# V/K stage: each turn of modulation rows is joined to the next block's first two chunks

## What is computed

```python
m = silu(c) @ w_ada + b_ada                  # (2048) @ (2048, 6*2048): shift, scale, gate, twice
h = rms_norm(x, g_pre) * (1.0 + scale) + shift
z = h @ w_in                                 # (2048, 4096): q | k | v | u
q, k = rotary(q), rotary(k)
attn = diff_attend(q, k, v, ...)             # prompt, and samples over cached pages
pooled = pool_mix(u, ...)
m = concatenate([rms_norm(attn) * ..., pooled]) @ w_out
x = x + gate * rms_norm(m, g_post)
x = x + gate2 * rms_norm(square(relu(h2 @ w1)) @ w2, g_post2)
```

## Time and profile before

| | |
|---|---|
| median of 3 runs | 1468.08 us (1467.49 to 1468.85) |
| profiled execution | 1467.77 us |
| its span | 1466.1 us |
| TensorE busy, share of the span | 1433.8 us, 98% |
| VectorE busy | 814.9 us, 56% |
| ScalarE busy | 524.8 us, 36% |
| bytes moved by DMA | 319.06 MB, mean 218 GB/s |
| mean granted TensorE clock | 0.995 |

### The profile page before, as it was taken

One profiled execution on the slowest core, in us unless ns is written; L12 is line 12 of the kernel. 1 busy time (PEld: TensorE's weight loads), 2 busy tenths in 40 slices (PEclk: granted clock), 3 DMA queues, 4 the chain that ended last, 5 costly groups with the idle time before them and its releaser, 6 DMA issues.

```text
span 1466.1 us, 26898 instructions
## 1 busy us (share of the span) xinstructions
PE 1433.8 (98%) x10278; PEld 1316.6 (90%) x10278; DVE 814.9 (56%) x1312; ACT 524.8 (36%) x753; POOL 115.4 (8%) x195
## 2 busy tenths in 40 slices
PE   6999999999999999999999999999999999999996
PEld 2788877888688879999999999999999999999996
DVE  5667668757555678664434554343554334555554
ACT  4333243443435644333222333332333322333331
POOL 1111000266210000000000000000000000000002
PEclk9999999999999999999999999999999999999998
DMA  9999888787799777334346334446443443334421
GB/s 374 342 340 341 331 311 314 276 310 281 282 349 347 280 269 300 144 143 172 143 165 238 144 143 157 159 144 239 156 151 144 152 161 146 144 143 144 149 109 72
DMA packets 88459, 319.06 MB, mean 218 GB/s; under 512 B 12240, under 2 KB 12496, under 8 KB 87744
## 3 DMA queue, kind: packets, MB, share of 16 engines
q1 hardware_dynamic: 79776, 290.49, 53.4%
q0 software_dynamic: 5360, 25.14, 4.6%
q10 hardware_dynamic: 3248, 2.39, 0.5%
HBM read 312.18 MB, written 5.80 MB: 217 GB/s over the span
## 4 chain that ended last, share of the span: by engine, by line
PE 93%; DVE 3%; DMA 1%; POOL 1%; issue 1%; ACT 1%; SPq 0%; POOLq 0%; ACTq 0%; DVEq 0%
PE bank L1572 74%; PE bank L1625 8%; PE bank L1549 3%; PE bank L1534 2%; PE bank L1897 2%; DMA raw<-in_stream 1%; PE bank L1812 1%; DVE w_lo L812 1%; PE bank L1743 1%; PE bank L1559 0%; PE bank L1842 0%; PE bank L1698 0%; PE bank L1524 0%; SPq L371 0%; ACT w_hi L418 0%
## 5 line engine op out<-in xcount | busy, mean ns | idle before, releaser
L418 ACT ACTIVATE w_hi<-raw 128x1024 fp32r<-128x1024 f32 x352 | 361.6, 1053 | 271.8 <-PE bank L1572 232.0
L812 DVE TENSOR_TENSOR w_lo<-raw,w_hi 128x1024 fp32r<-128x1024 f32 x352 | 419.6, 1226 | 40.9 <-ACT w_hi L418 38.6
L1572 PE MATMUL bank<-m_hi,w_hi 128*128 128x320 f32 x1280 | 397.2, 310 | 0.0
L1572 PE MATMUL bank<-m_hi,w_lo 128*128 128x320 f32 x1280 | 395.5, 309 | 0.0
L1572 PE MATMUL bank<-m_lo,w_hi 128*128 128x320 f32 x1280 | 395.5, 309 | 0.0
L1572 PE MATMUL bank<-h_hi,w_hi 128*128 128x320 f32 x1216 | 378.7, 311 | 0.0
L1572 PE MATMUL bank<-h_hi,w_lo 128*128 128x320 f32 x1216 | 375.7, 309 | 0.0
L1572 PE MATMUL bank<-h_lo,w_hi 128*128 128x320 f32 x1216 | 375.7, 309 | 0.0
L1572 PEld LDWEIGHTS bank<-m_hi,w_hi 128*128 128x128 f32 x1280 | 240.3, 188 | 12.0 <-issue 12.0
L1572 PEld LDWEIGHTS bank<-h_hi,w_hi 128*128 128x128 f32 x1216 | 228.3, 188 | 13.9 <-issue 13.8
L1572 PEld LDWEIGHTS bank<-m_lo,w_hi 128*128 128x128 f32 x1280 | 240.3, 188 | 0.0
(11 more groups left out here) (240 smaller groups left out, 1130.3 us busy)
## 6 DMA issues: line engine op xcount, KB each, us to landing
raw<-in_stream SPq DMA_DIRECT2D x544, 512.0 KB, 4.3
k_pages<-in_kc POOLq DMA_DIRECT2D x16, 512.0 KB, 6.4
v_pages<-in_vc POOLq DMA_DIRECT2D x16, 512.0 KB, 5.4
x<-in_x_cm SPq DMA_DIRECT2D x4, 640.0 KB, 6.8
x_mid<-in_x_cm POOLq DMA_DIRECT2D x1, 2560.0 KB, 10.0
x<-in_x_cm POOLq DMA_DIRECT2D x1, 2560.0 KB, 13.8
v_out<-v_cm POOLq DMA_DIRECT2D x1, 1280.0 KB, 9.5
k_out<-back POOLq DMA_DIRECT2D x1, 1280.0 KB, 6.0
```

Source lines behind the costliest of these rows:

```text
L418: act.activation(w_hi[2 * (j % 2) + h][:, :], raw[slot][:, h * 1024:(h + 1) * 1024], ACT.Copy).then_inc(hi_ready, 1)
L812: dve.tensor_tensor(w_lo[q][:, :], raw[slot][:, h * 1024:(h + 1) * 1024], w_hi[q][:, :], ALU.subtract).then_inc(slot_used[slot], 1)
L1572: last = pe.matmul(bank[j % 2][:, 0:T], w[q][:, k * P:(k + 1) * P], v[:, 8 * h + k, :], start=(h == 0 and k == 0 and n == 0), stop=(h == 1 ...
```

## The change

The turn of block n + 1 and chunks 0 and 1 of block n + 2 become one visit. TensorE's order in slice n after: V half 0; chunks 2 and 3 of block n + 1; V half 1 whole; turn of block n + 1 and chunks 0 and 1 of block n + 2 (in the last slice: and the first chunk of block 9); K half 0; K half 1. Block 1's first two chunks now lie before the first slice. The stream is laid out to match: block 0, chunks 0 and 1 of block 1, then for each slice the V chunk, chunks 2 and 3, the K chunk, chunks 0 and 1 of the block after. `keep_clock` before the stage has 4 matmuls, not 8.

```diff
-SLICED = [0, 3, 6, 9]
-SLICED_ADA = [[1, 2, 4, 5], [7, 8, 10, 11]]
+SLICED = [2, 5, 8, 11]
+SLICED_ADA = [[3, 4, 6, 7], [9, 10, 12, 13]]
...
-            ada_copy(n + 1, quarter_use(n // 2), SLICED_ADA[n % 2][3])
+            ada_copy(n + 1, quarter_use(n // 2), SLICED_ADA[n % 2][1])
...
         ada_turn(0)
-        keep_clock(bank[5], 8)
+        keep_clock(bank[5], 4)
+        for a in range(2):
+            ada_chunk(1, quarter_use(0), a, a)
...
                 nb, places = 2 * g + (i + 1), SLICED_ADA[i]
-                ada_chunk(nb, use, places[0], 0)
-                ada_chunk(nb, use, places[1], 1)
                 pe.wait_ge(h_ready, 2 * g + (i + 1))
                 slice_tiles(i, 0, 0, range(4))
-                slice_tiles(i, 0, 1, range(2))
-                ada_chunk(nb, use, places[2], 2)
-                ada_chunk(nb, use, places[3], 3)
-                slice_tiles(i, 0, 1, range(2, 4))
+                ada_chunk(nb, use, places[0], 2)
+                ada_chunk(nb, use, places[1], 3)
+                slice_tiles(i, 0, 1, range(4))
                 ada_turn(nb)
-                slice_tiles(i, 1, 0, range(4))
-                slice_tiles(i, 1, 1, range(2))
                 if last and i == 1:
                     nb, place, a = fill_ada(0)[0][0]
                     ada_chunk(nb, fill(0)[1], place, a)
-                slice_tiles(i, 1, 1, range(2, 4))
+                else:
+                    ada_chunk(nb + 1, use, places[2], 0)
+                    ada_chunk(nb + 1, use, places[3], 1)
+                slice_tiles(i, 1, 0, range(4))
+                slice_tiles(i, 1, 1, range(4))
...
-    chunks = ada_block(0)
-    for g in range(QUARTERS):
-        products = [slice_chunk(w_in, 2 * g + i, vk[8 * jj:8 * jj + 8]) for i in range(2) for jj in range(2)]
-        chunks += place(products, SLICED, (2 * g + 1, 2 * g + 2))
+    chunks = ada_block(0) + ada_block(1)[:2]
+    for n in range(SLICES):
+        chunks += [slice_chunk(w_in, n, vk[:8])] + ada_block(n + 1)[2:] + [slice_chunk(w_in, n, vk[8:])]
+        if n + 1 < SLICES:
+            chunks += ada_block(n + 2)[:2]
```

## The result

The changed kernel takes 1469.62 us (median of 20 runs, 1467.96 to 1472.23), the kernel before 1468.07 us (20 runs, 1466.61 to 1471.46). The forecast was 1470.4 us, 0.16% more.

The account below looks back on a forecast made before the run. TensorE, carrying 93% of the chain, bounds the kernel. Profiled 1467.77 us plus 2.3 lost at the stage's start, less 8 x 0.00 for the join, gives 1470.1; the runs' median lies 0.3 higher: 1470.4 us, range 1468.4 to 1472.4.

Parts of the forecast that it names:

- Joined visit at the price of its parts: V/K stage slices: turn plus two chunks cost joined what they cost apart, 0.44 and 2.03 us; saving 0.00, 8 times.
- The 0.08 a slice for the turn's exit: Skill's tiling-mode drain rule: joining spares only the gap behind the turn, about 0.6 us in all, sum 1.7 us.
- The lone chunk of block 9 joins at 0.00: Last slice: one chunk of block 9 joining the turn changes the cost by 0.00.
- Bank 0 at 40.6: First slice: K half lands at 37.7, split and first sum take 2.83 us, so bank 0 is free at 40.6.
- step 3: Start of stage, TensorE: products and chunks to about 37.5, idle to 40.6, next slice's first product 53.6, before 51.27.
- 3.1 us with nothing: First slice: TensorE idle from about 37.5 until bank 0 is free at 40.6.
- the rival: Clock falls near 32: free, the wait to 40.6 swallows it; after the second idle time 1.0 to 1.7 us; chance 0.15.
- Loss 2.3 us at the start: Start of stage: second slice's first product at 53.6 instead of 51.27, 2.3 us lost and not given back.
- A cure of the bank wait would return 1.2: First slice without the bank wait: block 2's second chunk would be 1.9 us late, so only 1.2 us returns.
- keep_clock at 0: Before the stage: four fewer small matmuls, ahead of later-landing data, cost 0; not over 1 us without that cover.
- Steady slack 0.4 us, cost 0: Steady slices: the next slice's first tile wants bank 0 after 7.04 us, free at 6.6; slack 0.4 us, no loss.
- (a): Steady slices: three halves of products (72 matmuls, 10.6 us) run without a visit; bank 0 slack 0.4 us, cost 0.

Follow-up runs that it names:

- split_join: Changed kernel with the first K tile (6 matmuls) put between the turn and the next block's two chunks, undoing the join; 1469.07 us, ratio 1.0004.
- chunks_first: Changed kernel with the order inside the joined visit swapped, chunks ahead of the turn; 1470.29 us, ratio 1.0015.
- sums_first: Changed kernel, but in slice 0 VectorE drains the banks of V half 0 before splitting the first K half; 1470.26 us, ratio 1.0010.
- sums_and_clock: Changed kernel with VectorE draining slice 0's banks before the K split, plus 14 more small matmuls in TensorE's first gap; 1470.05 us, ratio 1.0012.
- four_in_one: Kernel before with all four modulation chunks of the next block in one visit at the slice's head, turn alone; 1478.26 us, ratio 1.0065.

## Why the prediction was right, point by point

- **Joined visit at the price of its parts.** Right to 0.02 us: 2.47 against 0.45 + 2.04 in split_join. The 0.08 a slice for the turn's exit (0.6 in all, for a sum of 1.7) did not come either. Most slices are of 18.58 in the joined and in the split kernel, and their times do not differ beyond the noise. That the drain between transposes and 32-column chunks is what takes the gain was argued from 0.53 against 0.35 us; chunks_first, which turns that border round, found the same total but for 0.04, so the mechanism stays argued.
- **The lone chunk of block 9 joins at 0.00.** Its own work did cost nothing (split_join and the changed kernel show no wait for it), but the step priced the work alone and not the landing: the chunk is wanted right behind the turn, at 174.29 in the changed kernel and at 177.77 before. In four of the seven traces with this stream it was waited for, 0.3 to 1.0 us.
- **First product 32.0.** 32.30. Right.
- **Bank 0 at 40.6.** 39.6 in the one trace, 40.4 in the other, by the landing of the K half (36.77 and 37.57; expected 37.7). The chain from landing to bank, 2.83 us, was right: 36.77 to 39.6. The other execution had the whole wait for VectorE that step 3 describes, only shorter.
- **3.1 us with nothing.** Wrong as drawn: 0.28 and 1.16 us. The clock fell at about 32, as the rival had it, and took up the gap, at no cost in these two, as the rival said too. In split_join and sums_first it lasted twice as long and was not free: V half 1 started at 40.49 with its bank free.
- **Loss 2.3 us at the start.** 1.50 and 2.30 in the changed kernel's two traces; the estimate took the K half at the later of its two places.
- **A cure of the bank wait would return 1.2.** It returned 0.63 with the clock kept as well. The place was nearly right: 53.6 - 1.2 = 52.4 for the second slice's first product, and it was 55.75 - 3.61 = 52.14; the return is smaller because the changed kernel's own place is 52.77 and not 53.6. The later expectation of sums_and_clock, 51.7, missed that a chunk whose halves land apart costs twice its time (below): it had the products going on 0.5 us behind the landing, and it was 1.0.
- **keep_clock at 0.** Not tested by itself; the first gap of 4 us lowers the clock with four matmuls ahead of it, and with eight before there was no such gap.
- **Steady slack 0.4 us, cost 0.** Nearly: 0.44 us in seven slices together. It was not (a) as drawn, behind K half 1, but one half earlier: VectorE splits the next V half before it sums K half 0, and that V half is met 2.6 to 3.4 us behind the turn. Only at 3.4 (102.42, behind the turn at 99.00) did TensorE wait for the bank between the K halves for 0.2 us.
- **Total.** 1469.6 for 1470.4, and that it is so near is in part luck. The stage lost 1.86 and 3.03 us in the two traces, more than the medians' 1.55. In the first trace 1.14 us of it came back around 530 us, where the kernel before had run at the low clock and the changed one had not; the forecast did not count on it. How often either happens, the times without a trace can't tell.

## What to carry to other kernels

Price a join by a place in the trace where the two already stand next to each other; the gaps at the borders of the separate ones may simply move inside. When work is pulled forward in a stream that is saturated, write down for each piece the place that it needs in the stream: every place is a landing time, and the last piece that the first dense stretch needs sets its start, here 2.6 us a chunk. The same holds at the other end: a lone chunk that is used earlier must also land earlier. And an idle gap is judged by what comes behind it: a fall of the clock that is absorbed by a later wait is free as long as it takes no more than that wait is long, and filling the first of two gaps moved the fall behind the second, where it cost 1.5 us.

## What the runs showed of the hardware

- The four matmuls of a modulation chunk, each into its own 32 partitions, take 0.85 us together. When the wait for the second half splits them, each half takes as long as the whole: a row of one half (x4) lasts 1.03 and that of a whole chunk (x8) 1.04. That the four run at once when nothing splits them is the reading that fits; nothing here shows it more directly. In the kernel before a chunk and one half take 37.00 to 39.04 less the wait of 0.15:

```profile
37.00 1.89 PE L1534 MATMUL bank<-raw,silu_c 128*9 128x512 f32 x12
```

  12 records (a chunk and a half) in 1.89 us are as long as 16 (two chunks, 1.91). In sums_and_clock the same, 1.96 for 12. In four_in_one a second 0.85 for the split fourth chunk and a wait of 0.2 make the 1.07 us over the expected visit.
- Behind the gap of 4 us the slow clock (1.2 GHz) lasted 3.4 us in two traces of the changed kernel and about twice that in three others: 6.9 us in split_join, 6.3 us of it from 32 to 40, and 6.8 in sums_first and chunks_first. In these three it had begun to fall before 32 (0.93, 0.89 and 0.86 from 28 to 32), in the two others it had not (1.00). split_join:

```profile
32.00:36.00 4.00, 3.78 (x14) 3.79 (x15) 3.99 (x3) 0.00 (x0) 0.00 (x0) 0.50 1.04 408
36.00:40.00 4.00, 4.00 (x28) 2.80 (x26) 2.11 (x4) 1.99 (x2) 0.00 (x0) 0.71 0.87 345
```

  TensorE was busy all through it (3.78 of the first 4 us, then 4.00). What decides between the two lengths is open. Whether it spreads the times is not shown either: the kernel before has no such gap in this stage, and its 20 runs are spread over 4.9 us.
